# Attention units taken two at a time in TensorE's order of a two-layer hybrid decoder trunk

## The reference

```python
x = layer_norm(alpha * x + 0.5 * swiglu(x, ...))
y = token_mix(x, ...)          # concat[NSA(4 heads), sliding-window(4 heads), HGRN2(4 heads)] @ w_out
x = layer_norm(alpha * x + y)
# banded_attention, per block of 128 queries:
s = einsum('bqhgd,bkhd->bhgqk', qi, kk) * scale; s = where(mask, s, NEG_INF)
pr = softmax(s)                                    # with a sink column for the sliding-window heads
out = einsum('bhgqk,bkhd->bqhgd', pr, vv)
# nsa: o = g0 * o_cmp + g1 * o_slc + g2 * o_win    (compressed keys, selected blocks, window)
```

## Time and profile before

| what | value |
|---|---|
| median of 3 runs | 2207.23 us (2207.04 to 2210.95) |
| profiled execution, whole | 2208.09 us |
| profiled execution, span of the engines | 2206.2 us |
| PE busy | 2176.4 us, 99% of the span |
| DVE busy | 1133.1 us, 51% |
| ACT busy | 903.0 us, 41% |
| granted TensorE clock | 1.000 |
| chain that ended last | PE 92%, ACT 4%, DVE 3%, issue 1%, DMA 1% |

### The profile page before, as it was taken

The page is one execution under the profiler, slowest core; times in us unless marked ns, Lnnn a source line. Parts: engine busy times, 40 slices in busy tenths (PEclk is TensorE's granted clock), DMA queues, the critical chain, the costliest instruction groups (busy, mean ns, idle before and its releaser), DMA issues.

```text
span 2206.2 us, 30817 instructions
## 1 busy us (share of the span) xinstructions
PE 2176.4 (99%) x12675; PEld 1801.2 (82%) x12675; DVE 1133.1 (51%) x1968; ACT 903.0 (41%) x1449; POOL 137.5 (6%) x128
## 2 busy tenths in 40 slices
PE   9999999999999999999999999999999999999999
PEld 7888888887668888888888888898876788888888
DVE  4333344898857333343643333358988663333454
ACT  4223223656646322222532222256576463222244
POOL 0000011220000000011000000112200100000110
PEclk9999999999999999999999999999999999999999
DMA  5333333332223333332333333333322233333332
GB/s 169 99 101 97 89 96 91 100 79 58 82 72 87 96 96 96 102 94 85 102 96 97 100 99 87 98 82 100 86 75 62 60 104 96 96 96 105 89 89 72
DMA packets 384220, 202.76 MB, mean 92 GB/s; under 512 B 17361, under 2 KB 381777, under 8 KB 384081
## 3 DMA queue, kind: packets, MB, share of 16 engines
q1 hardware_dynamic: 383520, 200.15, 31.9%
q10 hardware_dynamic: 560, 0.66, 0.1%
HBM read 198.68 MB, written 2.10 MB: 91 GB/s over the span
## 4 chain that ended last, share of the span: by engine, by line
PE 92%; ACT 4%; DVE 3%; issue 1%; DMA 1%; POOL 0%; SPq 0%; DVEq 0%; ACTq 0%
PE banks L254 27%; PE banks L256 27%; PE banks L255 27%; ACT xhi L353 1%; PE banks L1524 1%; ACT xT L354 1%; PE banks L1511 1%; PE banks L1465 1%; PE banks L311 1%; PE banks L305 1%; PE banks L1008 1%; PE banks L306 1%; ACT w_hi L240 0%; PE banks L1012 0%; ACT lev L1720 0%
## 5 line engine op out<-in xcount | busy, mean ns | idle before, releaser
L246 DVE TENSOR_TENSOR w_lo<-w_raw,w_hi 128x1024 fp32r<-128x1024 f32 (+2 forms) x370 | 451.0, 1222 | 814.2 <-ACT w_hi L240 814.0
L254 PE MATMUL banks<-xhi,w_hi 128*128 128x512 f32 (+1 forms) x1936 | 757.2, 391 | 1.5 <-DVE w_lo L246 1.5
L256 PE MATMUL banks<-xhi,w_lo 128*128 128x512 f32 (+1 forms) x1936 | 748.9, 387 | 0.0
L255 PE MATMUL banks<-xlo,w_hi 128*128 128x512 f32 (+1 forms) x1936 | 748.7, 387 | 0.0
L240 ACT ACTIVATE w_hi<-w_raw 128x1024 fp32r<-128x1024 f32 (+2 forms) x370 | 375.9, 1018 | 811.8 <-PE banks L256 796.5
L254 PEld LDWEIGHTS banks<-xhi,w_hi 128*128 128x128 f32 x1936 | 365.0, 189 | 75.9 <-DVE w_lo L246 2.0
L256 PEld LDWEIGHTS banks<-xhi,w_lo 128*128 128x128 f32 x1936 | 363.5, 188 | 74.4
L255 PEld LDWEIGHTS banks<-xlo,w_hi 128*128 128x128 f32 x1936 | 363.8, 188 | 72.7 <-issue 1.0
L254 PE MATMUL banks<-hhi,w_hi 128*128 128x512 f32 (+1 forms) x792 | 293.4, 371 | 0.0
L256 PE MATMUL banks<-hhi,w_lo 128*128 128x512 f32 (+1 forms) x792 | 289.5, 365 | 0.0
L255 PE MATMUL banks<-hlo,w_hi 128*128 128x512 f32 (+1 forms) x792 | 289.4, 365 | 0.0
(11 more groups left out here) (276 smaller groups left out, 1990.8 us busy)
## 6 DMA issues: line engine op xcount, KB each, us to landing
w_raw<-in_ffn_w_gu_dram SPq DMA_DIRECT2D x176, 512.0 KB, 3.9
w_raw<-in_ffn_w_down_dram SPq DMA_DIRECT2D x64, 512.0 KB, 4.0
w_raw<-in_w_in_dram SPq DMA_DIRECT2D x48, 512.0 KB, 4.1
w_raw<-in_ffn_w_down_dram SPq DMA_DIRECT2D x32, 384.0 KB, 3.5
w_raw<-in_w_out_dram SPq DMA_DIRECT2D x32, 256.0 KB, 2.9
w_raw<-in_ple_gate_w_dram SPq DMA_DIRECT2D x16, 512.0 KB, 3.8
w_raw<-in_cmp_k_w_dram SPq DMA_DIRECT2D x16, 256.0 KB, 2.8
w_raw<-in_cmp_v_w_dram SPq DMA_DIRECT2D x16, 256.0 KB, 3.1
```

Source lines behind the costliest of these rows:

```text
L246: dve.tensor_tensor(part_view(wlo, n), raw_view(split_at[n]).rearrange("p k n -> p (k n)"), part_view(whi, n), ALU.subtract).then_inc(sems ...
L254: pe.matmul(bank, w_hi, x_hi, start=first, stop=False)
L255: pe.matmul(bank, w_hi, x_lo, start=False, stop=False)
L256: return pe.matmul(bank, w_lo, x_hi, start=False, stop=last)
```

## The change

From turn 4 to turn 23 PE takes the turns in pairs. A pair (n, n+1) issues the values of units n-4 and n-3, the score products of units n+1 and n+2, their masks, then the transposes of unit n-2, `compressed(n)`, pieces, the transposes of unit n-1, `compressed(n+1)`, pieces. Where only the second turn of a pair has an output piece, its first half goes between the two transposes and its second half behind the second. Turns 0 to 3 and 24 to 27 keep their order. The turns of three steps of the compressed branch are one earlier, on all three engines, and five output pieces are one turn later. The sequences on ACT and DVE are otherwise the same.

```diff
-        HID_ODD, HID_SUM, HID_ACT, HID_DVE, HID_TURN, KC_TURN, SC_TURN, PCT_TURN = 4, 5, 6, 7, 9, 10, 11, 14
+        HID_ODD, HID_SUM, HID_ACT, HID_DVE, HID_TURN, KC_TURN, SC_TURN, PCT_TURN = 4, 5, 6, 7, 8, 9, 10, 14
+        ALONE = 4
-        CHUNK_TURNS = (5, 6, 7, 12, 16, 18, 20, 22)
+        CHUNK_TURNS = (5, 6, 7, 13, 17, 19, 21, 23)
         SPLIT_TURNS = (3, 4, 5, 10, 14, 16, 18, 20, 21, 22, 23, 24)
...
         def scores(pe, layer, n):
+            score_products(pe, layer, n)
+            score_masks(pe, layer, n)
...
-            def chunk(n):
+            def chunk(n, ks=range(KH)):
                 c = CHUNK_TURNS.index(n)
+                first, last = ks[0] == 0, ks[-1] == KH - 1
...
-                elif n == SC_TURN + 1:
+                elif c == 3:
                     pe.wait_ge(*upto("sc_sub", layer, 1))
-                elif n == PCT_TURN + 2:
+                elif c == 4:
                     pe.wait_ge(*upto("pct_out", layer, 1))
...
+            def two_turns(n):
+                in_halves = n + 1 in CHUNK_TURNS and n not in CHUNK_TURNS
+                values(n - 4)
+                values(n - 3)
+                score_products(pe, layer, n + 1)
+                if n + 2 < UNITS:
+                    score_products(pe, layer, n + 2)
+                score_masks(pe, layer, n + 1)
+                if n + 2 < UNITS:
+                    score_masks(pe, layer, n + 2)
+                turn(n - 2)
+                compressed(n)
+                if n in CHUNK_TURNS:
+                    chunk(n)
+                if in_halves:
+                    chunk(n + 1, range(KH // 2))
+                turn(n - 1)
+                compressed(n + 1)
+                if in_halves:
+                    chunk(n + 1, range(KH // 2, KH))
+                elif n + 1 in CHUNK_TURNS:
+                    chunk(n + 1)
...
-            for n in range(UNITS + 4):
-                if n >= 4:
-                    values(n - 4)
-                if n + 1 < UNITS:
-                    scores(pe, layer, n + 1)
+            for n in range(ALONE):
+                scores(pe, layer, n + 1)
                 compressed(n)
-                if n in CHUNK_TURNS:
-                    chunk(n)
-                if 2 <= n < UNITS + 2:
+                if n >= 2:
+                    turn(n - 2)
+            for n in range(ALONE, UNITS, 2):
+                two_turns(n)
+            for n in range(UNITS, UNITS + 4):
+                values(n - 4)
+                if n < UNITS + 2:
                     turn(n - 2)
```

More of the change, by code:

```diff
@@ L1448, in scores, with score_products @@
         def scores(pe, layer, n):
+            score_products(pe, layer, n)
+            score_masks(pe, layer, n)
+        def score_products(pe, layer, n):
             kind, g, i, k0 = units[n]
@@ L1457, in scores @@
             w_ = width(n)
-            wm = w_ if kind == SWA else P
             for hh in range(2):
@@ L1465, in scores, with score_masks @@
                 pe.matmul(ps[:, score_bank(n) + hh, 0:w_], qs, proj[half(hh), ks, k0 * P:(i + 1) * P], start=True, stop=False)
+        def score_masks(pe, layer, n):
+            w_ = width(n)
+            wm = w_ if units[n][0] == SWA else P
             for hh in range(2):
@@ L1579, in chunk @@
                     pe.wait_ge(*upto("half_done", layer, c))
-                multiply(pe, w0 + c, 7, lambda k: xhi[:, KH + k, :], lambda k: xlo[:, KH + k, :])
+                multiply(pe, w0 + c, 7, lambda k: xhi[:, KH + k, :], lambda k: xlo[:, KH + k, :],
+                         first=first, last=last, ks=ks, finish=last)
             def att_piece(a, ks, bank, first=True, last=True):
@@ L1615, in means @@
                 mm.then_inc(sems["mean_mm"], 1)
-            compressed(-1)
-            for n in range(UNITS + 4):
-                if n >= 4:
-                    values(n - 4)
-                if n + 1 < UNITS:
-                    scores(pe, layer, n + 1)
+            def two_turns(n):
[9 more added lines that the diff above has]
+                turn(n - 2)
                 compressed(n)
@@ L1625, in heads_pe @@
                     chunk(n)
-                if 2 <= n < UNITS + 2:
+                if in_halves:
[6 more added lines that the diff above has]
+                    chunk(n + 1)
+            compressed(-1)
+            for n in range(ALONE):
[8 more added lines that the diff above has]
+                if n < UNITS + 2:
                     turn(n - 2)
```

## The result

The changed kernel takes 2233.9 us (2230.1 to 2234.6) against 2207.3 us: a ratio of 1.0111, with a 95% interval of 1.0098 to 1.0124. The ratio is taken over the single executions, four of each kernel here; the quotient of the two medians is 1.0120. I had forecast 2221.5, with a range of 2211 to 2228. The direction was right, but the loss is 24.5 us by the ratio (26.6 by the medians), 1.7 to 1.9 times the 14.2 that I said. All ratios are of fast executions alone: one of the eleven of the kernel with pairs from turn 16, at 2403.2 us and a granted clock of 0.85, was a slow one.

What follows compares the result with a forecast made beforehand. PE was taken to set the pace. Per layer, 15.8 us new waits, less 4.7 old waits and 4.5 shape changes, plus 0.5 for half pieces, gave 7.1 more; two layers 14.2, so 2221.5 us, range 2211 to 2228.

Steps and rivals of the forecast that it cites:

- What bounds the kernel: Layer one, `values(0)` to unit 22's transposes: PE sets the pace, busy 67.79 of 72.59 us; its waits are paid in full.
- the prices of the shapes: On PE, each pair pays three changes of shape (0.08, 0.15, 0.22 us) once: 4.5 us less a layer.
- The waits: PE's new waits on ACT and DVE: 15.8 us a layer, 7.3 from pair 12's chain; 4.7 us of old ones go.
- rival 1: Clock falls to 1.2 GHz in pair 12, up to 3.9 us more a layer: 2225.5, at most 2229; chance 0.27.
- rival 2: On PE, changes of shape cost the same in pairs, so the 4.5 us don't come: 2230 us; chance 0.05.
- rival 3: PE's waits are half the sum, 8 us a layer: 2206 us, within 0.2% of before; chance 0.10.
- Rival 4: In pair 10, compressed scores reach DVE before anything queues behind them, sparing pair 12's 7.3 us: 2200.6 us; chance 0.05.

Runs made afterwards that it cites:

- the waits filled: The changed kernel with idle matmuls put where PE waited, in pairs 8, 10, 12 and 14: 2223.0 us, ratio 1.0062 to the kernel before.
- the old turns: The changed kernel, still in pairs, with the three moved compressed-branch steps back at turns 9, 10, 11: 2222.2 us, ratio 1.0061.

## Why the prediction was wrong

**What bounds the kernel, and the prices of the shapes: right.** The groups of two units show 0.15 and 0.22 us once where they stood twice.

**The waits: right, nearly one by one.** At full clock the stretch of layer one took 79.33 us against 79.7 forecast. In the profile after, `values(8)` waited 4.29 us (4.2 forecast), the transposes of unit 13 2.0 (2.1), those of unit 7 1.17 (1.4), the scores of unit 22 0.67 (0.8). `values(7)` waited 1.10 us with its predecessors at half the clock and 1.48 where they ran at full clock (1.7). The scores of unit 14 waited 1.54 us and not 3.1 only because the products ahead of them ran at half the clock and ended later; they started 4.39 us behind the group output, where the sum said 4.4. `values(13)`, given 0.5, did not wait in layer one of the profile after, and 0.3 us in other kernels.

**The step that failed is the choice between the forecast and rival 1, and rival 1's price.** I took the clock to stay at 2.4 GHz (0.53) because the trace of before showed it there under waits of up to 1.3 us. That premise does not hold. These are the longest wait of before, then two places of the profile after:

```profile
640.92 1.06 PE L1511 MATMUL banks<-ident,lev 128*128 128x128 f32 x8 [1.33 <-ACT lev L1711]
```

```profile
592.54 1.04 PE L1532 MATMUL banks<-lev,v_tok 128*64 128x128 f32 x8
...
1674.98 0.66 PE L1532 MATMUL banks<-lev,v_tok 128*64 128x128 f32 x8 [1.48 <-ACT lev L1746]
```

The clock fell at 592.6, during the values of unit 6 (1.04 us where they last 0.66): behind one wait of 1.17 us, shorter than the 1.33 under which before kept it, and ahead of the next one (1.10 us). The longest single wait of the earlier trace rows was no measure of the risk.

The mechanism of rival 1 was right and the price was mis-sized. I priced only what follows in pair 12, 2 us a layer with 3.9 as the end. The clock was down from 592.6, ahead of pair 12, to 613.1 with one break of 3.4 us, and again in pair 16. The whole stretch of layer one took 84.27 us against 79.33 with the waits filled, 4.9 us for the clock: 3.7 of them from the start of pair 8 to that of pair 14 (29.35 against 25.68), 1.15 from there to pair 18 (15.44 against 14.29), 0.1 ahead. In layer two it was 4.5 us. With rival 1 at that price the sum is 2221.5 + 9.4 = 2230.9, outside my range; the measured ratio gives 2231.8 on the 2207.3 us of before. Of the 10.8 us that go with the fills this leaves 1.4 unexplained, within the spread of either kernel (4 to 5 us).

The Trainium skill, TensorE: Matmul & The Clock Gate, HAM oscillation, warns of idle gaps between bursts of matmuls. The traces agree in that idle time of PE stood ahead of every fall, and that the clock stayed up through the attention stages once all those waits were filled. They don't agree with a reading by the longest gap: the fall at 592.6 had 1.17 us behind it, while a wait of 1.48 us at `values(1)` of layer two (to 1674.98) in the same profile left the clock at 1.00.

**Rivals 2, 3 and 4 fall.** The changes of shape are saved (pair 6 above, and pairs from 16 are faster), and at full clock the waits came to their sum, not to half of it. Rival 4's idea, that the compressed scores reach DVE before it has anything to queue, is what the kernel with the maximum behind the group output tried from the other side: it gives back at most 3.8 us of 24.5, not a gain.

**What the pairs are worth** where no queue meets them: 0.17% for four pairs a layer, 1.9 us a layer (2.2 in the sum, of which 1.8 for the changes of shape).

What stays open is what decides when the clock falls. The lower clock in pair 16 of layer one (623.4 to 626.8) stands behind a wait of 2.00 us. It is gone when that wait is filled, but other waits were filled too; and the same wait of 2.00 us leaves the clock up in layer two of the same profile (to 1726.55) and in both layers of the kernels with the old turns and with the maximum behind the output. And whether idle matmuls at turns 2 and 3 really narrow the spread, and why not the median, was not tried further.

## What to carry to other kernels

Joining two iterations on the busiest engine saves what stands between groups of different shapes, and it takes away the distance that hid the other engines' latency; add up, for each consumer in the new order, its producer's queue since the last hand-off. Where a step of another engine waits in the middle of a fixed order, whatever stands behind it in that order waits too, so a step that comes early on one engine can come too early on the next. If the sum leaves TensorE with more idle time than before, price its following work at the lower clock, and try idle matmuls in the waits as the first experiment: they separate the two effects. They cost nothing as long as the clock stays up; where it fell ahead of them, 24 records lasted 4.60 us in place of 2.94 and ran 1.5 us over the wait that they were to fill.

## What the runs showed of the hardware

The clock fell to 1.2 GHz behind a wait of 1.17 us (592.6 in the profile after), and stayed at 2.4 GHz under single waits of 1.33 us (640.9 in the profile before), 1.48 and 2.00 us (layer two of the profile after). With only pair 12 filled it fell at 594.8 and stayed down for 13.7 us although PE was busy for 12.09 of them. Fifteen idle matmuls a layer in the shorter waits made the changed kernel 6.0 us faster, thirty-eight 10.8 (0.5%); twenty-three in pair 12 alone 2.4, which is not clear of the spread. At the lower clock what streams takes nearly twice as long (2.08 us for four score records of 512 columns against 1.13), and ACT and DVE keep their pace: the compressed maximum and what follows it to the group output took 4.3 us at either level (601.34 to 605.66 in the profile after, 595.95 to 600.28 with the waits filled).
